# Issuing the SBUF-to-SBUF exchange transfers of a two-layer decoder trunk from ScalarE in place of SyncE

## The reference

```python
h = jnp.einsum('btd,de->bte', x, w_in)
...
x1, x2 = xr[..., :half], xr[..., half:]
rot = jnp.concatenate([x1 * cos - x2 * sin, x2 * cos + x1 * sin], axis=-1)
```

## Time and profile before

| | |
|---|---|
| median of 3 runs | 805.83 us (804.8 to 807.54) |
| the profiled execution | 805.21 us |
| its span, first to last instruction | 803.6 us |
| PE busy | 779.5 us, 97% |
| DVE busy | 545.4 us, 68% |
| ACT busy | 392.9 us, 49% |
| POOL busy | 91.2 us, 11% |
| chain that ended last | PE 86%, DVE 5%, DMA 3%, ACT 2%, SP's queue 1% |

### The profile page before, as it was taken

The page is one execution under the profiler, slowest core; times in us unless marked ns, Lnnn a source line. Parts: engine busy times, 40 slices in busy tenths (PEclk is TensorE's granted clock), DMA queues, the critical chain, the costliest instruction groups (busy, mean ns, idle before and its releaser), DMA issues.

```text
span 803.6 us, 16797 instructions
## 1 busy us (share of the span) xinstructions
PE 779.5 (97%) x6314; PEld 723.1 (90%) x6314; DVE 545.4 (68%) x1008; ACT 392.9 (49%) x773; POOL 91.2 (11%) x166
## 2 busy tenths in 40 slices
PE   8999899999999999999999979999999999999995
PEld 7998598888889999999869978888888999999994
DVE  4565378987679675656465675888876876665664
ACT  5443156666465544443345531666656464444423
POOL 2341441000123200000000014410000000000000
PEclk9999999999999999999999998999999999999998
DMA  8988467533777766555437765666338366565621
GB/s 306 284 277 281 125 207 250 206 105 103 239 266 241 244 184 183 178 176 173 131 101 243 253 193 179 211 211 211 104 118 304 121 184 184 184 183 178 176 94 54
DMA packets 41689, 153.62 MB, mean 191 GB/s; under 512 B 6288, under 2 KB 7312, under 8 KB 40976
## 3 DMA queue, kind: packets, MB, share of 16 engines
q1 hardware_dynamic: 33312, 114.24, 45.8%
q0 software_dynamic: 8304, 38.37, 14.0%
HBM read 145.77 MB, written 13.34 MB: 198 GB/s over the span
## 4 chain that ended last, share of the span: by engine, by line
PE 86%; DVE 5%; DMA 3%; ACT 2%; issue 1%; SPq 1%; DVEq 0%; ACTq 0%
PE bank L648 22%; PE bank L649 21%; PE bank L650 21%; DMA ring<-weights_dram 3%; PE bank L859 3%; PE bank L666 3%; PE bank L809 1%; DVE w_lo L1162 1%; PE bank L659 1%; PE bank L815 1%; PE bank L980 1%; PE bank L900 1%; PE bank L989 1%; PE bank L839 1%; PE bank L789 1%
## 5 line engine op out<-in xcount | busy, mean ns | idle before, releaser
L1162 DVE TENSOR_TENSOR w_lo<-ring,w_hi 128x1024 fp32r<-128x1024 f32 x202 | 248.3, 1230 | 152.7 <-ACT w_hi L998 148.8
L648 PE MATMUL bank<-x_hi,w_hi 128*128 128x264 f32 x1208 | 349.5, 289 | 1.7 <-DVE w_lo L1162 1.7
L650 PE MATMUL bank<-x_lo,w_hi 128*128 128x264 f32 x1208 | 342.5, 284 | 0.0
L649 PE MATMUL bank<-x_hi,w_lo 128*128 128x264 f32 x1208 | 342.4, 283 | 0.0
L998 ACT ACTIVATE w_hi<-ring 128x1024 fp32r<-128x1024 f32 x202 | 213.0, 1055 | 69.8 <-PE bank L650 34.3
L648 PEld LDWEIGHTS bank<-x_hi,w_hi 128*128 128x128 f32 x1208 | 227.5, 188 | 5.9 <-issue 3.4
L649 PEld LDWEIGHTS bank<-x_hi,w_lo 128*128 128x128 f32 x1208 | 227.8, 189 | 0.3
L650 PEld LDWEIGHTS bank<-x_lo,w_hi 128*128 128x128 f32 x1208 | 226.8, 188 | 0.0
L648 PE MATMUL bank<-h_rounded,w_hi 128*128 128x264 f32 x352 | 102.2, 290 | 0.0
L649 PE MATMUL bank<-h_rounded,w_lo 128*128 128x264 f32 x352 | 100.2, 285 | 0.0
L1050 ACT ACTIVATE h<-bank 128x264 f32<-128x264 f32 x88 | 34.6, 393 | 105.1 <-PE bank L650 96.5
(11 more groups left out here) (240 smaller groups left out, 947.1 us busy)
## 6 DMA issues: line engine op xcount, KB each, us to landing
ring<-weights_dram SPq DMA_DIRECT2D x208, 512.0 KB, 3.7
cache_a<-kcmp_dram POOLq DMA_DIRECT2D x32, 128.0 KB, 3.6
cache_b<-vcmp_dram POOLq DMA_DIRECT2D x32, 128.0 KB, 3.6
cache_a<-ksel_dram POOLq DMA_DIRECT2D x32, 128.0 KB, 2.7
cache_b<-vsel_dram POOLq DMA_DIRECT2D x32, 128.0 KB, 2.8
cache_a<-kwin_dram POOLq DMA_DIRECT2D x2, 2048.0 KB, 12.6
cache_b<-vwin_dram POOLq DMA_DIRECT2D x2, 2048.0 KB, 9.3
kv_dram<-h POOLq DMA_DIRECT2D x2, 1584.0 KB, 7.6
```

Of the source, the lines that this page charges most:

```text
L648: pe.matmul(out, w_high[:, k0 + k, :], high, start=(k == 0), stop=False)
L649: pe.matmul(out, w_rest[:, k0 + k, :], high, start=False, stop=False)
L650: ins = pe.matmul(out, w_high[:, k0 + k, :], rest, start=False, stop=(k == kn - 1))
L1162: dve.tensor_tensor(w_lo[:, slot % RING], ring[:, slot % RING], w_hi[:, d % HI_RING].bitcast(F32), ALU.subtract).then_inc(w_lo_ready, 1)
```

## The change

The function `swap` moves unchanged from SP's program into ACT's. SP now only loads weights, parameters and inputs and stores the output. ACT calls `swap(l, i - 1)` right behind its own eviction of `dense` i, for the same eight pairs in each layer. The transfers, the places they read and write, their semaphores and all waits are the same.

```diff
-SWAP_AFTER = {SLOT_OF[l, "dense", n + 1]: (l, n) for l in range(DEPTH) for n in [KC, VC] + ROPE_PAIRS}
...
                     sp.wait_ge(slots_done, RING + before + 1)
                 load(slice(n, n + 1), n)
-                if before in SWAP_AFTER:
-                    swap(*SWAP_AFTER[before])
...
+            def swap(l, first):
+
+                for n in (first, first + 1):
+                    wait_emptied(act, l, "dense", n)
+                if first in ROPE_PAIRS:
+                    u = ROPE_PAIRS.index(first)
+                    if u == 0:
+                        act.wait_ge(z_clear, 1)
+                    if 2 <= u < 4:
+                        act.wait_ge(roped, l * len(ROPED) + 2 * (u - 1))
+                    if u >= 4:
+                        act.wait_ge(cmp_in_ready, 2 * l + u - 3)
+                    dst = ROPE_Z[u]
+                    for at in (0, 8, HD, HD + 8):
+                        to = at + 8 if at % HD == 0 else at - 8
+                        act.dma_start(z[to:to + 8, dst:dst + 2, :], h[at:at + 8, first:first + 2, :]
+                                     ).then_inc(rope_landed[u], 16)
...
                             emptied_by(ins, step, i)
+                            if i - 1 in [KC, VC] + ROPE_PAIRS:
+                                swap(l, i - 1)
```

More of the change, by code:

```diff
@@ L454, in load @@
                                     ).then_inc(landed[i % RING], 16)
[L456 to L479, removed]
             load(slice(0, 1), 0)
@@ L998, in round_weight @@
                 act.activation(w_hi[:, d % HI_RING], ring[:, slot % RING], ACT.Copy).then_inc(w_hi_ready, 1)
+            def swap(l, first):
[14 more added lines that the diff above has]
+                                     ).then_inc(rope_landed[u], 16)
+                else:
+                    if first == KC:
+                        act.wait_ge(z_clear, 1)
+                    dst = 4 if first == KC else 6
+                    for at in (0, HD):
+                        act.dma_start(z[HD - at:2 * HD - at, dst:dst + 2, 0:SEQ], h[at:at + HD, first:first + 2, 0:SEQ]
+                                     ).then_inc(own_landed[first // VC], 16)
             act.wait_ge(landed[0], 16)
```

## The result

The changed kernel took 815.83 us (median of four runs, 815.3 to 818.74), the kernel before 806.68 us in the same measurement (804.8 to 807.81). The ratio is 1.012, with a 95% interval of 1.0101 to 1.0139: 9.2 us slower. The forecast was 811.3 us, 5.5 us slower, in a range of 807.5 to 816.0. So the sign was right, and the size was too small by 3.7 us. The profiled execution of the changed kernel is the slowest of its four runs (818.74 us, span 817.1). Sums are made with that profile.

What follows compares the result with a forecast made beforehand. The prediction took PE's work plus its waits to bound the kernel. Layer 0's 2.2 us and layer 1's 3.2 us, with the clock at 0, made 5.4 us: 811.3 us, range 807.5 to 816.

Steps and rivals of the forecast that it cites:

- late rounding: On ACT, a swap's requests delay the next rounding, hence DVE's `w_lo` and then PE; forecast 5.4 us in all.
- The clock: PE's clock: 1.7 us may come back at layer 0's `gates`, each `dense` 13 wait may cost 1.7; taken as 0.
- If the clock falls elsewhere: One of the signs that the prediction is wrong: PE's clock falling at other places than forecast; no size given.
- The end of layer 1: From `dense` 18 to `gates` of layer 1: last rotation, `gate_d` and `gates` come 3.2 us late, halves landed in time.
- What bounds the kernel: Whole kernel: time is PE's work plus its waits; ACT or SP changes count only through those waits.
- 2.9 us late per four-transfer swap: On ACT behind an eviction: four requests take 2.7 us, so ACT is free after 3.2 us instead of 0.29.
- cheap rival: Chance 0.12: a request on ACT takes 0.33 us, four 1.3; about 1.5 to 2.3 us lost, 807.7 us.
- Layer 1, `dense` 13: The `kw` swap delays the rounding for `dense` 10 and DVE's gapless run, so PE waits 2.9 us at `dense` 13.
- Layer 0: `dense` 13 comes 3.05 us later, part swallowed before `gates`; the layer loses 1.4 to 2.4 us, taken as 2.2.
- The gain from SP's earlier loads: SP, free of swaps, asks for the load behind `dense` 18 of layer 1 0.28 us earlier.
- the other side: Chance 0.06: ACT's arithmetic passes its requests and SP's loads leave earlier, gaining 0.6 to 2.3 us: 804.0.
- Dearer requests: Chance 0.14: requests collide or are slowed, four take 3.8 us, both `dense` 13 waits drop the clock; 816.9 us.

Runs made afterwards that it cites:

- after_again: The changed kernel as it is, measured a second time: 814.04 us, ratio 1.0129 to the kernel before.
- last_l1: The kernel before with only the last swap (behind `dense` 19) of layer 1 on ACT: 809.54 us, ratio 1.0037.
- behind_rounding: The kernel before with seven swaps of a layer on ACT, each behind the next rounding, the last left on SP: 805.24 us, ratio 0.9995.
- mid_only: The kernel before with only the swaps behind `dense` 13, 15 and 17 on ACT: 806.22 us, ratio 1.0002.
- kw_back: The changed kernel with the `kw` swap (behind `dense` 7) given back to SP: 809.17 us, ratio 1.0043 to the kernel before.
- last_only: The kernel before with only the last swap of each layer (behind `dense` 19) on ACT: 809.48 us, ratio 1.0047.
- no_swaps: The kernel before with no swap transfers asked for by any engine, so values differ from the reference: 804.25 us, ratio 0.9973.
- kw_only: The kernel before with only the `kw` swap (behind `dense` 7) of each layer on ACT: 814.43 us, ratio 1.0107.
- before_kv_late: The kernel before with POOL's store of keys and values asked for behind its `ksel` loads: 802.02 us, ratio 0.9952.
- last_only_kv_late: The kernel before with each layer's last swap on ACT and POOL's key and value store behind its `ksel` loads: 806.37 us, ratio 1.0021.

## Why the prediction was right or wrong

The mechanism of the late rounding was right, and the size was too small. In order of time, by PE's first matmuls of `dense` 13 and of `gates` in after_again:

| | forecast | after_again |
|---|---|---|
| layer 0, to the first evictions of layer 1 | 2.2 us | 2.3 us |
| layer 1 up to `dense` 13 | 2.9 us | 2.9 us |
| from there to `gates` | 0.3 us | 2.8 us |
| behind `gates` | 0 | 0.8 us |
| sum | 5.4 us | 8.8 us |

On the median of 805.83 the 5.4 us are 811.2, which the prediction has as 811.3.

These are the lines of after_again in layer 1 (PE, DVE, PE), next to 450.56, 479.07 and 483.21 before:

```profile
455.77 0.39 PE L620 MATMUL bank<-x_hi,w_hi 128*128 128x264 f32 x1 [2.08 <-DVE w_lo L1161]
...
486.85 0.71 DVE L1242 TENSOR_TENSOR z<-z,cst 128x528 f32<-128x528 f32 x1 [0.34 <-DMA z<-h]
...
491.23 0.59 PE L697 MATMUL bank<-cst,gate_d 48*128 48x3 f32 x2 [3.60 <-DVE gate_d L1230]
```

**The clock** is the step that failed, as the prediction put it: "Between -1.7 and +3.4 I take 0." In after_again it is +1.7 behind `dense` 13 of layer 0, -1.7 behind `gates` of layer 0, where the fall of before is missing, +1.7 behind `dense` 13 of layer 1, and +0.8 for the longer stretch around its `gates`, where PE works at low clock for 5.7 us (491.23 to 497.0) and before for 4.1 (483.21 to 487.3). Together these are +2.5 us of the 3.4 by which the sum of 5.4 fell short. In layer 0 the two terms cancel, as the 0 had it; in layer 1 nothing stands against them. I took a value near the middle of two ends, although a wait of 2.26 us had been followed by a fall and the two new waits were forecast as long; the +1.7 of each had more for it than the 0. That the low stretch around `gates` of layer 1 could grow was in no term. "If the clock falls elsewhere" was also one of the prediction's own signs of being wrong.

Counted the other way, PE's waits add 5.7 us for `w_lo` and take 1.6 around `gates`, +4.1, and the clock +2.5. That makes 6.6 of the 8.8 us between the spans (812.4 - 803.6); 2.2 us are not assigned. In the slower profile the clock makes up 6.2 us of 13.5.

**The end of layer 1** was mis-sized too. The term was 3.2 us, of which 0.3 was this swap's own. Between `dense` 13 and `gates` after_again loses 2.8 us, of which 1.7 are the fall of the clock, so 1.1 are left for this end; by itself in layer 1 the last swap costs 3.0. One step of it failed: "The halves, 1.98 us behind the last request, have landed by then". In the changed order SP's weight loads run beside the swap, and the halves take 3.4 to 4.0 us. DVE waits for them 0.34 us in after_again and 0.86 in last_l1. The rivals had named a collision of transfers for the requests, but not for the landing.

**What bounds the kernel** held. The change neither adds nor speeds up arithmetic, and the time moved by PE's waits and what follows them.

**2.9 us late per four-transfer swap** held: four requests in 2.61 us, median 0.632, the `kw` rounding 2.90 us late in layer 1. Requests can run beside arithmetic that has begun: in behind_rounding they ran beside a rounding. But a rounding behind them in the stream started after the last of them in every trace. The Trainium skill's sentence in "DMA: Bandwidth & Descriptors", section "Issuing engines are not separate DMA queues", says that transfers run on the same 16 engines whichever engine starts them, and that asking from several engines saves only the time to initiate, usually small beside the transfer. The first part fits the halves, which landed later beside the weights. The second does not hold here: one request took 0.632 us and the last transfer landed 2.0 to 4.0 us after its request began, and the place of four requests decided 8.6 us. The prediction's sentence that by this rule the time would stay near 805.8 "as in the cheap rival" is a slip, since that rival's own sum is 807.7.

**Layer 1, `dense` 13** held. DVE's run is a block of 11.71 us, and PE waits 2.08 us there in both profiles. PE's first matmul of `dense` 13 in layer 1 of after_again is 5.2 us later than before, and the evictions of that layer's first tiles were 2.3 us later: 2.9 us come from this place, as forecast. That the swaps of 13, 15 and 17 cost nothing by themselves held in mid_only. The `kc`, `vc` and `ks` swaps were not run alone; kw_back, which holds them, the middle three and the last, costs no more than last_only (3.5 and 3.8 us).

**Layer 0** held for `dense` 13: PE begins at 49.84 where it began at 47.64, and both profiles after run 0.3 to 0.6 us ahead at the first evictions. PE's wait before `dense` 8 came to 0.67 us, taken as 1.0. ACT's timeline and POOL's store of the slower profile:

```profile
67.28 0.54 POOL L525 DMA_DIRECT2D kv_dram<-h  x1 [0.30 <-issue]
...
67.55 4.38 ACTq L988 DMA_DIRECT2D z<-h  x4
...
78.13 1.06 ACT L970 ACTIVATE w_hi<-ring 128x1024 fp32r<-128x1024 f32 x1 [4.76 <-DMA ring<-weights_dram]
...
79.54 2.61 ACTq L988 DMA_DIRECT2D z<-h  x4
82.25 1.06 ACT L970 ACTIVATE w_hi<-ring 128x1024 fp32r<-128x1024 f32 x1 [2.79 <-issue]
```

The rounding for 21 starts at 78.13, forecast at 75.2, and that for 22 at 82.25, forecast at 79.4. Both are 2.9 us later than the sum had; in after_again they are 1.6 and 1.5 us later (76.81 and 80.94), about the 1.7 of the fall behind `dense` 13, which the sum left out. The wait before `gates` swallowed part: PE's `gates` came 4.0 us later in after_again (87.36 against 83.39), above the 2.4 at the top, and the missing fall behind it gave back 1.7. That last part is as the prediction had it: a wait of 0.39 us, and no fall. So the 2.3 us beside the forecast 2.2 rest on two clock terms that happened to cancel.

**The gain from SP's earlier loads**, 0.28 us, was rightly small: no_swaps puts all that SP can give at about 2 us.

**The rivals.** Cheap requests and the other side fell with the median of 0.632. Dearer requests were not the cause either, though its time (816.9) lies near the measured one: requests at `kw` and at the end of layer 1 took their 2.6 us, and only the swap of `ks` in layer 0 (3.26) and the one beside POOL's store (4.38) took over 3. But one part of this rival came true, that both waits at `dense` 13 drop the clock. The side on which SP's freed loads leave earlier was real, but it cost where the rival let it gain: the loads reached the transfer engines beside the halves. So the measured 815.83 lies inside the recorded range of 807.5 to 816.0 only because its upper end was stretched for this rival; it is above the 814.8 at which the forecast's own range ended.

**What stays open.** Seven of the 18 profiles have a low stretch of the clock that begins between 102 and 113 us, with no idle time of PE ahead of it that I found. after_again has none there, the slower profile has one:

```profile
112.00:116.00 4.00, 4.00 (x23) 4.00 (x23) 3.46 (x6) 0.00 (x0) 1.62 (x3) 0.60 0.38 110
```

Why some waits of 2 to 3 us are followed by a fall and others are not is open too. Nor is it settled how the swaps' two losses cover each other: kw_only and last_only sum to 12.4 us, and the whole change cost 9 to 10. And no engine was tried for the exchange itself; that transfers make it is how this kernel is written.

## What to carry to other kernels

A transfer's request is work on the engine that asks for it: four small ones at 0.63 us were 2.6 us, almost a whole step of PE, so put them behind the instruction that others wait for, not ahead of it. The four requests of the `kw` swap cost 8.6 us behind the eviction; with six other swaps, behind the rounding, they cost nothing. Look at how long an engine is idle at that place and at how many instructions run without a gap behind it; the share of its busy time (48% for ACT) tells neither. And count a new wait of PE for itself and, where low clock follows, once more, some 1.7 us here. A fall that is avoided can come back at the next wait.

## What the runs showed of the hardware

- Requests from ACT ran while ACT's arithmetic that had begun before them was still under way (437.13 inside 436.94 to 437.99, behind_rounding), but the next arithmetic behind four requests started at least 0.04 us after the last of them in all 15 traces with such requests.
- Beside POOL's store of keys and values four requests took 4.38 us from ACT, and 4.45 in last_only, in place of 2.6; before, the same happened to SP with 3.82. With the store moved, SP's swap took 2.65 us (before_kv_late) and ACT's 3.21 (last_only_kv_late).
- Over 28 runs of the kernel before, the mean granted clock goes with the time: 0.990 with a median of 805.1 us (15 runs), 0.988 with 807.1 us (9 runs). That fits one more or one fewer low stretch, some 2 us each. Two traces of last_only show such a difference: one low stretch at 805.0 us, four at 810.61.
- The same four small transfers landed 1.98 us after the last request with the transfer engines at a share of 0.32, and 3.96 us after it at 0.77.
- Waits of PE of 2.07 and 2.08 us were followed by a low stretch of 3.4 us at `dense` 13 (after_again, both layers), and one of 2.07 us was not (kw_only, layer 0).
- Filling a wait of PE in layer 0 moved the fall of the clock to the next wait and left the time as it was (813.87 and 814.04 us).
